# Plain fp32 products in column groups for the tokens over 128 of two gathered experts

## The reference

```python
def moe_ffn(u, w_router, b_router, w_gate, w_up, w_down):
    ...
    for e in range(N_EXPERTS):
        h = jax.nn.silu(u @ w_gate[e]) * (u @ w_up[e])
        y = y + gates[..., e:e + 1] * (h @ w_down[e]).astype(F32)
```

## Time and profile before

| | |
|---|---|
| median of 3 runs | 1476.37 us (1475.01 to 1477.93) |
| the profiled execution, its own time | 1475.07 us |
| its span | 1473.3 us |
| TensorE busy | 1402.8 us, 95% |
| VectorE busy | 807.9 us, 55% |
| ScalarE busy | 555.7 us, 38% |
| mean granted TensorE clock | 0.978 |
| mean DMA rate | 186 GB/s |
| ranks 2 and 3 | about 1048 to 1240 us of the span |
| ranks 4 to 7 | about 1240 to 1445 us |

### The profile page before, as it was taken

How to read it: one execution, slowest core, us unless ns; L and a number is a source line. 1 busy time by engine, 2 the same in 40 slices (tenths; PEclk the granted TensorE clock), 3 DMA queues, 4 the chain that set the end, 5 groups by cost and what they waited for, 6 DMA issues and landing times.

```text
span 1473.3 us, 20621 instructions
## 1 busy us (share of the span) xinstructions
PE 1402.8 (95%) x8551; PEld 1153.3 (78%) x8551; DVE 807.9 (55%) x1284; ACT 555.7 (38%) x721; POOL 23.6 (2%) x79
## 2 busy tenths in 40 slices
PE   6999999979999998999996999999999999999996
PEld 3678777679999966878774999999777676876664
DVE  1566315364444456641447534645545556899994
ACT  2351111154333235311104433334334345677762
POOL 6000000000000000000000000000000000000000
PEclk8999999989999999999997999999999999999999
DMA  9543764765545553445341724635656457999970
GB/s 321 180 143 126 250 200 152 260 196 172 159 152 165 171 160 114 144 160 189 112 126 44 242 90 154 220 104 180 196 177 205 148 188 230 315 343 339 353 245 32
DMA packets 205009, 274.75 MB, mean 186 GB/s; under 512 B 7783, under 2 KB 136065, under 8 KB 204916
## 3 DMA queue, kind: packets, MB, share of 16 engines
q1 hardware_dynamic: 192928, 262.57, 54.3%
q10 hardware_dynamic: 11988, 10.86, 2.3%
HBM read 267.11 MB, written 6.30 MB: 186 GB/s over the span
## 4 chain that ended last, share of the span: by engine, by line
PE 87%; DVE 7%; DMA 2%; ACT 2%; issue 1%; SPq 1%; DVEq 0%; ACTq 0%
PE bank L1002 17%; PE bank L871 10%; PE bank L873 9%; PE bank L872 9%; PE bank L901 8%; PE bank L902 8%; PE bank L903 8%; PE bank L949 2%; PE bank L1083 2%; PE bank L1095 1%; DMA out_dram<-SD 1%; PE bank L957 1%; PE bank L1091 1%; DMA raw<-in_w_ada_dram 1%; PE bank L1201 1%
## 5 line engine op out<-in xcount | busy, mean ns | idle before, releaser
L660 DVE TENSOR_TENSOR lo_raw<-raw,hi 128x2048 fp32r<-128x2048 f32 (+2 forms) x112 | 229.6, 2056 | 129.6 <-ACT hi L1487 129.0
L1487 ACT ACTIVATE hi<-raw 128x2048 fp32r<-128x2048 f32 (+2 forms) x112 | 193.5, 1728 | 136.0 <-PE bank L903 105.8
L1002 PE MATMUL bank<-UM,raw 128*128 128x288 f32 x896 | 228.2, 411 | 0.0
L871 PE MATMUL bank<-UH,hi 128*128 128x288 f32 x704 | 210.2, 299 | 9.2 <-DVE UL L1847 7.6
L1002 PEld LDWEIGHTS bank<-UM,raw 128*128 128x128 f32 x896 | 169.5, 192 | 50.3 <-issue 6.0
L873 PE MATMUL bank<-UL,hi 128*128 128x288 f32 x704 | 207.9, 295 | 0.0
L901 PE MATMUL bank<-hi,UGH 128*96 128x512 f32 (+7 forms) x384 | 144.5, 376 | 1.5 <-DVE XHF L2348 1.5
L903 PE MATMUL bank<-hi,UGL 128*96 128x512 f32 (+7 forms) x384 | 143.6, 374 | 0.0
L871 PEld LDWEIGHTS bank<-UH,hi 128*128 128x128 f32 x704 | 132.9, 189 | 9.5 <-issue 9.5
L873 PEld LDWEIGHTS bank<-UL,hi 128*128 128x128 f32 x704 | 133.3, 189 | 0.0
L872 PE MATMUL bank<-UH,lo 128*128 128x288 f32 x432 | 128.2, 297 | 0.0
(11 more groups left out here) (411 smaller groups left out, 2360.7 us busy)
## 6 DMA issues: line engine op xcount, KB each, us to landing
raw<-in_w_ada_dram SPq DMA_DIRECT2D x48, 1024.0 KB, 5.8
raw<-in_w_in_dram SPq DMA_DIRECT2D x28, 1024.0 KB, 7.7
raw<-in_w_exp_gate_dram SPq DMA_DIRECT2D x26, 1024.0 KB, 5.3
raw<-in_w_exp_up_dram SPq DMA_DIRECT2D x26, 1024.0 KB, 5.3
raw<-in_w_exp_down_dram SPq DMA_DIRECT2D x16, 1024.0 KB, 5.3
raw<-in_w_exp_down_dram SPq DMA_DIRECT2D x16, 768.0 KB, 4.6
raw<-in_w_ff_gate_dram SPq DMA_DIRECT2D x11, 1024.0 KB, 5.5
raw<-in_w_ff_up_dram SPq DMA_DIRECT2D x11, 1024.0 KB, 5.4
```

The lines of the kernel that those rows point to most:

```text
L660: dve.tensor_tensor(lo_x[g % XRAW][:, 0:XG[g][2] * XG[g][3]], x_raw(g), hi_x[g % XSPLIT][:, 0:XG[g][2] * XG[g][3]].bitcast(F32), ALU.subtr ...
L871: pe.matmul(out, wh, xh, start=start, stop=False)
L1002: mm = pe.matmul(bank[t][:, 0:N], w_[:, d, t * P:t * P + P], x_, start=(d == 0), stop=(d == KT - 1))
L1487: act.activation(hi_x[q][:, 0:XG[g][2] * XG[g][3]], x_raw(g), ACT.Copy).then_inc(S("x_hi_made"), 1)
```

## The change

The token tiles of ranks 2 and 3 are cut anew: a full tile of 128 tokens and a rest of 64 (rank 2, `SPREAD` 2) or 32 (rank 3, `SPREAD` 4; `CAPS` grows from 144 to 160). The full tile is computed as before. The rest is computed in plain fp32 from `raw` and from `UG` or `HRX` directly, without a split: the weight columns of a block are dealt over two groups of 64 or four groups of 32 array columns (`columns`), so that a k step is two matmuls of 256 moving columns or four of 128.

- `rest_block(g + 2)` is issued on TensorE before block g, since `x_lo` later overwrites `raw`. `x_lo` of these blocks waits for `rest_mm` and moves from step g - 3 to step g - 2 of VectorE (`lows_due`).
- The rest has its own Silu (ScalarE, steps 0, 4, 8), multiplication (VectorE, steps 2, 6, 10), transposes (`turn_rest`, after b = 3, 7, 11) and copy to `HRX` (ScalarE, steps 4, 8, 12). `boxes` gives the rectangles of the spread-out layout.
- `slot_masks` makes `ST` and `GSL` of the rest once for each group; `scatter` reads the rest from partitions 0, 32, 64 or 96 on.
- For all gathered experts `scatter` moves from after blocks 1, 4, 7, 10 to after 0, 2, 4, 6, and `add_slots` from steps 2, 5, 8, 11 to 1, 3, 5, 7.
- `UG` grows from 702 to 718 columns. The split of the tokens (`UGH`, `UGL`, `HHX`, `HLX`) covers the full tile only.

The diff, cut to its core:

```diff
 CAPS = [c + c % 2 for c in CAPS]
 SLOTS = []
 SLOT_OFF = {}
+SPREAD = []
 for _r in range(DENSE, NE):
     SLOT_OFF[_r] = sum(w_ for _, _, w_ in SLOTS)
-    _parts = -(-CAPS[_r] // P)
-    for _i in range(_parts):
-        SLOTS.append((_r, SLOT_OFF[_r] + _i * (CAPS[_r] // _parts), CAPS[_r] // _parts))
+    _rest = CAPS[_r] - P
+    assert _rest <= P // 2
+    SLOTS.append((_r, SLOT_OFF[_r], min(P, CAPS[_r])))
+    SPREAD.append(1)
+    if _rest > 0:
+        _rest = P // 4 if _rest <= P // 4 else P // 2
+        CAPS[_r] = P + _rest
+        SLOTS.append((_r, SLOT_OFF[_r] + P, _rest))
+        SPREAD.append(P // _rest)
...
+def columns(i, w_):
+    step = 512 // SPREAD[i]
+    return [(a, min(a + step, w_)) for a in range(0, w_, step)]
...
+REST = [g for g, t in enumerate(XG) if t[0] >= DENSE and len(TILES[t[0]]) > 1]
+REST_AHEAD = 2
+def lows_due(g):
+    return [x for x in (g + 2, g + 3) if x < NX and x - g == (2 if x in REST else 3)]
...
+            if g in REST:
+                dve.wait_ge(S("rest_mm"), REST.index(g) + 1)
             dve.tensor_tensor(lo_x[g % XRAW][:, 0:XG[g][2] * XG[g][3]], x_raw(g),
...
+            def rest_block(g):
+                r, b, kk, w_ = XG[g]
+                rs = r - DENSE
+                i = TILES[r][1]
+                n_ = SLOTS[i][2]
+                pe.wait_ge(S(f"x_full{g % XRAW}"), 16 * (g // XRAW + 1))
+                if g == REST[0]:
+                    pe.wait_ge(S("gb_made"), DENSE)
+                    pe.wait_ge(S("x_up_read"), DENSE * XCB)
+                if b < SUP:
+                    ci, up, half = b // 4, b // 2 % 2, b % 2
+                    x_, to = UG[:, 4 * half:4 * half + 4, SLOTS[i][1]:SLOTS[i][1] + n_], 2 * up + 1
+                    first, last = half == 0, half == 1
+                    if first and up:
+                        pe.wait_ge(S("rest_hf_made"), 3 * rs + ci)
+                    elif first:
+                        pe.wait_ge(S("rest_sg_made"), 3 * rs + ci)
+                        if ci == 0:
+                            pe.wait_ge(S("slot_hl_made"), 3 * rs)
+                            pe.wait_ge(S("rest_hx_made"), 3 * rs)
+                else:
+                    h, q = DOWN[b - SUP]
+                    x_, to = HRX[:, 4 * q:4 * q + kk, P:P + n_], (5 if h else 7)
+                    first, last = q == 0, q == 2
+                    pe.wait_ge(S("rest_hx_made"), 3 * rs + q + 1)
+                    if first and h == 0:
+                        pe.wait_ge(S("y_scaled"), DENSE * XDB)
+                        pe.wait_ge(S("sc_read"), 4 * rs)
+                    elif first:
+                        pe.wait_ge(S("slot_hl_made"), 3 * rs + 2)
+                w = x_raw(g).rearrange("p (k n) -> p k n", k=kk)
+                for k in range(kk):
+                    for q, (c0, c1) in enumerate(columns(i, w_)):
+                        mm = pe.matmul(bank[to][n_ * q:n_ * q + n_, 0:c1 - c0], x_[:, k, :], w[:, k, c0:c1],
+                                       start=first and k == 0, stop=last and k == kk - 1)
+                mm.then_inc(S("rest_mm"), 1)
+            def rest_due(g):
+                if g + REST_AHEAD in REST:
+                    rest_block(g + REST_AHEAD)
...
                         for c in range(NTT):
-                            pe.transpose(bank[6 + i % 2][0:w_, c * TT:c * TT + TT],
-                                         OH[:, c, off:off + w_].bitcast(F32), ident[0:TT, 0:TT])
+                            for q in range(SPREAD[i]):
+                                if SPREAD[i] == 1:
+                                    pe.transpose(bank[6 + i % 2][0:w_, c * TT:c * TT + TT],
+                                                 OH[:, c, off:off + w_].bitcast(F32), ident[0:TT, 0:TT])
+                                else:
+                                    pe.matmul(bank[6 + i % 2][w_ * q:w_ * q + w_, c * TT:c * TT + TT],
+                                              OH[:, c, off:off + w_].bitcast(F32), ident[0:TT, 0:TT], start=True, stop=True)
                         for c in range(NTT):
-                            mm = pe.matmul(bank[6 + i % 2][0:w_, N:N + 1], OH[:, c, off:off + w_].bitcast(F32),
-                                           GATR[:, c, r:r + 1], start=(c == 0), stop=(c == NTT - 1))
+                            for q in range(SPREAD[i]):
+                                mm = pe.matmul(bank[6 + i % 2][w_ * q:w_ * q + w_, N:N + 1], OH[:, c, off:off + w_].bitcast(F32),
+                                               GATR[:, c, r:r + 1], start=(c == 0), stop=(c == NTT - 1))
...
+                        rest_due(g)
                         pe.wait_ge(S("x_lo_made"), g + 1)
...
-                            for t, i in enumerate(TILES[r]):
-                                _, off, w_ = SLOTS[i]
-                                at_ = (f % 2) * CAPS[r] + off - w0
-                                mm = pe.transpose(bank[(0 if ci == 2 else 4) + f // 2][:, at_:at_ + w_],
-                                                  HFX[0:w_, t, f * P:f * P + P], ident[0:w_, 0:w_])
+                            mm = pe.transpose(bank[b0 + f // 2][:, f % 2 * w_:f % 2 * w_ + w_],
+                                              HFX[0:w_, 0, f * P:f * P + P], ident[0:w_, 0:w_])
...
+                    def turn_rest(r, ci):
+                        rs = r - DENSE
+                        i = TILES[r][1]
+                        pe.wait_ge(S("rest_hf_made"), 3 * rs + ci + 1)
+                        if ci == 0:
+                            pe.wait_ge(S("ysl_made"), halves_of(2 * rs))
+                        if ci == 1:
+                            pe.wait_ge(S("slot_hl_made"), 3 * rs + 1)
+                            pe.wait_ge(S("rest_hx_made"), 3 * rs + 1)
+                        if ci == 2:
+                            pe.wait_ge(S("slot_sg_made"), 3 * rs + 3)
+                        for j, fs in enumerate(rest_tiles(i, ci)):
+                            w_ = SLOTS[i][2] * len(fs)
+                            mm = pe.transpose(bank[(0 if ci == 2 else 4) + j][:, 2 * P:2 * P + w_],
+                                              HFX[0:w_, 1, j * P:j * P + P], ident[0:w_, 0:w_])
+                        mm.then_inc(S("rest_turned"), 1)
...
+                        for i in TILES[r][1:]:
+                            w_ = SLOTS[i][2]
+                            for x, b in enumerate(banks):
+                                d = 2 * pair + x
+                                step = 512 // SPREAD[i]
+                                q, c = d % 4 * P // step * w_, d // 4 * step + d * P % step
+                                pe.matmul(bank[b][:, 0:N], YSH[q:q + w_, 1, c:c + P], ST[q:q + w_, i, :], start=False, stop=False)
+                                mm = pe.matmul(bank[b][:, 0:N], YSL[q:q + w_, 1, c:c + P], ST[q:q + w_, i, :],
+                                               start=False, stop=True)
                         mm.then_inc(S("sc_full"), 1)
...
+                            n_ = SLOTS[TILES[r][0]][2]
+                            mm = slot_tiles(bank[2 * up][0:n_, 0:w_], g, UGH[:, 4 * half:4 * half + 4, 0:n_],
+                                            UGL[:, 4 * half:4 * half + 4, 0:n_], half == 0, half == 1)
...
-                        if rs > 0 and b in (1, 4, 7, 10):
-
-                            pair = b // 3
+                        if rs > 0 and b in (0, 2, 4, 6):
+                            pair = b // 2
                             pe.wait_ge(S("ysl_made"), halves_of(2 * rs - (1 if pair < 2 else 0)))
                             if pair > 0:
                                 pe.wait_ge(S("sc_read"), 4 * (rs - 1) + pair)
                             scatter(r - 1, pair, (6, 7))
+                        if len(TILES[r]) > 1 and b in (3, 7, 11):
+                            turn_rest(r, (b - 3) // 4)
...
+                            for v, w_, src in turned(r, ci):
+                                mm = act.activation(HHX[:, v, w_], src, ACT.Copy)
                             mm.then_inc(S("slot_hh_made"), 1)
+                        if len(TILES[r]) > 1 and b in (4, 8, 12):
+                            ci = b // 4 - 1
+                            i = TILES[r][1]
+                            act.wait_ge(S("rest_turned"), 3 * rs + ci + 1)
+                            for j, fs in enumerate(rest_tiles(i, ci)):
+                                n_ = SLOTS[i][2]
+                                mm = act.activation(HRX[:, 4 * ci + fs[0]:4 * ci + fs[-1] + 1:4 // SPREAD[i], P:P + n_],
+                                                    bank[(0 if ci == 2 else 4) + j][:, 2 * P:2 * P + n_ * len(fs)].rearrange(
+                                                        "p (f w) -> p f w", f=len(fs)), ACT.Copy)
+                            mm.then_inc(S("rest_hx_made"), 1)
+                        if len(TILES[r]) > 1 and b in (0, 4, 8):
+                            ci = b // 4
```

(23 more changed lines are left out.)

119 lines of the change are left out of this document (63 added, 56 removed).

## The result

The changed kernel takes **1435.39 us** (1434.92 to 1437.23, 4 runs) against 1475.86 us for the kernel before on the same chip (1475.01 to 1477.93, 4 runs): ratio 0.9726, 95% interval 0.9709 to 0.9743 (here and below a ratio is the time over that of the kernel before on the same chip; the brackets behind it are its 95% interval). The profiled execution took 1434.92 us, its span is 1432.8 us at a mean granted clock of 0.982, so 40.5 us less in the span.

The account below looks back on a forecast made before the run. TensorE bounds ranks 2 and 3; in ranks 4 to 7 VectorE and DMA are near full too. Terms sum to -35.9 us from 1475.07: 1439.2, plus 1.3 for the median, rounded 1440; range 1430 to 1462 (1430 to 1452: chance 0.68).

Parts of the forecast that it names:

- Second tiles, -91.8: Ranks 2 and 3: the second token tile's matmuls go, 45.9 us of TensorE for each expert, -91.8 us for both.
- Rests, +15.0 and +30.1: Rest products over 70 k steps each: rank 3 at 0.214 us a step, +15.0 us; rank 2 at 0.43, +30.1 us.
- rival of serial groups: Rank 2's rest: the two groups of 64 don't run side by side, +30.1 us, 1470 us; chance 0.08.
- Visits, +11.2: Going into column groups and back costs 0.31 us for each of 36 rest blocks, +11.2 us (bounds 7 and 22).
- rival of dear visits: Going into column groups and back costs 0.7 us instead of 0.31, 44 times: 17 us more, 1457 us; chance 0.12.
- Wider loads, +2.0: Full tiles with 128 tokens: 5 ns more for each of the 420 matmuls that stay, +2.0 us (0 to 3).
- Transposes, 0: Ranks 2 and 3: 44 transposes go, 22 wide ones and 9 of the rest come, about 3 us each way, 0.
- Scatter, +2.5: Scatter of ranks 2 and 3: rest rows start at other partitions, 0.31 us for each of eight pair groups, +2.5 us.
- Masks and gather, +1.6: Dense stage masks repeated over groups, about +1.2 us; gather with 16 more columns, 0.3 us; together +1.6 us.
- The earlier scatter, -5.0: Ranks 4 to 7: earlier additions remove TensorE's 6.3 us of stops at block 12, -5.0 us (0 to -6.3).
- The start of rank 2, -1.5: TensorE's 1.48 us wait for the last dense results is filled by the rest of block 2, -1.5 us.
- The lead: Rests two blocks ahead: VectorE may be 5.7 us late before TensorE stops; rival, lead too short, 1522 us, chance 0.05.

Follow-up runs that it names:

- experiment 5: Changed kernel with the rest of rank 3 in two groups of 256 columns instead of four of 128: 1450.24 us, ratio 0.9821.
- experiment 4: Changed kernel with the rest blocks issued in pairs ahead of every second full block, 18 visits instead of 36: 1430.59 us, ratio 0.9692.
- experiment 8: Changed kernel with each rest block cut in two, two k steps ahead of the full block and the others behind it: 1443.89 us, ratio 0.9786.
- experiment 7: Changed kernel with four rest blocks per visit (down product in pairs), 12 visits, VectorE's low halves behind its rest multiplication: 1431.01 us, ratio 0.969.
- experiment 1: Kernel before with only the earlier scatter (after blocks 0, 2, 4, 6; additions at steps 1, 3, 5, 7): 1468.91 us, ratio 0.9955.
- experiment 2: Changed kernel with scatter and additions of ranks 4 to 7 back at their old blocks, rank 3 staying early: 1443.75 us, ratio 0.978.
- experiment 6: Changed kernel with rest blocks one block ahead of the full tile instead of two, their low halves one step later: 1437.43 us, ratio 0.9736.
- experiment 3: Changed kernel with all k steps of one column group before those of the next in a rest block: 1469.19 us, ratio 0.9955.

## Why the prediction was right, and where it was off

The forecast was 1440 with -35.9 us; it came to 1435.4, and the spans differ by 40.5. The likeliest case is the one that happened, by its own mechanism. Of the 4.6 us between the two sums, 3.1 are the scatter: the gain of its move was sized too small, and its new rows were charged too much. The others are small sizes and two differences outside the changed stages that nearly cancel by luck: the profiled execution was 2.1 us earlier than forecast at the first dense product, and lost 1.7 us behind the last expert.

**Second tiles, -91.8: right.** In ranks 2 and 3 TensorE's time, from start to start, divides like this:

| us | before | after |
|---|---|---|
| products of the full tiles (before: both tiles) | 183.68 | 96.88 |
| rest | 0 | 45.01 |
| transposes | 2.94 | 4.56 |
| scatter | 4.29 | 5.40 |
| sum | 190.92 | 151.85 |

The 96.88 hold 4.9 us of entries and exits of the rest blocks (17 x 0.087 + 33 x 0.104), so 92.0 for the products themselves, half of 183.68.

**Rests, +15.0 and +30.1: right.** 0.2175 and 0.43 us for a k step: 15.2 and 30.1 us. The straight line between 128 and 512 columns was the right reading, for two groups of 64 too. The rival of serial groups is out, by the profile of the changed kernel itself; experiment 5 shows that the width of the groups doesn't matter.

**Visits, +11.2: right.** 0.30 us each by experiment 4 and again by 8. Read from the rows directly it is 0.09 before, 0.16 inside (0.14 in rank 3) and 0.10 behind, 0.35 where a 512-column product stands on either side. Behind a scatter it is only some 0.15, the part inside, since the other two are paid there without a visit as well: in experiment 4 a scatter that ends in products of 64 rows is followed 0.09 late by a full product too, and that one takes 0.34. Of the 17 visits saved in experiment 4, 13 stood between full products, at 0.335 to 0.35, and 4 behind a scatter: 13 x 0.345 + 4 x 0.15 = 5.1. For all 36 that gives 32 x 0.345 + 4 x 0.15 = 11.6 us, an estimate, where 36 x 0.30 would be 10.8; the forecast lies between. Its 0.31 came from small fp32 products of another part of the kernel. So the rival of dear visits is out. The Trainium skill (TensorEngine Tiling (Array Packing), Key Properties) has the engine drain at a change of the tiling mode; a loss of that kind is there at every visit, though no run shows that it is the drain. The 0.47 us that the prediction estimated from the skill's figures is half as much again as was measured.

**Wider loads, +2.0: 0.** With a stationary tile of 128 tokens the 512-column matmuls still follow each other after 0.231 us. The 5 ns that the forecast read from rank 4 were not the width. That window of 5.64 us begins behind four transposes, and the edge is what it paid for:

```profile
1258.54 0.47 PE L901 MATMUL bank<-hi,UGH 128*116 128x512 f32 x1
1258.85 0.40 PE L902 MATMUL bank<-lo_raw,UGH 128*116 128x512 f32 x1
```

The first product takes 0.31 us, the 23 behind it (5.64 - 0.31)/23 = 0.232 each.

**Transposes, 0: right, though the table has +1.6.** A group of four wide ones takes 0.53 us there, up to the start of the rest block behind it:

```profile
1079.46:1079.99 0.53, 0.53 (x4) 0.36 (x3) 1.00 0.00 0
```

The end of such a group is not the transposes' own. The two of the rest take 0.31 us in the changed kernel, where a rest block follows. In experiment 7 a full product follows directly. There it starts 0.14 us behind the first of the two, and takes 0.32 itself:

```profile
1069.56:1069.87 0.31, 0.31 (x2) 0.14 (x1) 1.00 0.00 0
```

```profile
1072.88 0.38 PE L1517 MATMUL bank<-ident,HFX 128*128 128x128 f32 x2
1073.01 0.48 PE L954 MATMUL bank<-hi,UGH 128*128 128x512 f32 x1
1073.33 0.40 PE L955 MATMUL bank<-lo_raw,UGH 128*128 128x512 f32 x1
```

So 0.17 us at the end of each of the 12 turns, 2.1 in all, are the entry of the visit behind it, and a full product there would have paid 0.09 for the edge anyway. Less the 0.17, four wide transposes take 0.36 us, 0.09 each (an estimate: no run has a full product directly behind four wide ones), near the 0.083 of the forecast.

**Scatter, +2.5: +1.5.** The four pair groups of rank 2 take 1.36 us instead of 1.08, 0.28 for the change from 128 to 64 rows and back. Those of rank 3 stay at 1.09. There the stationary operands of the two 32-row products of a pair lie in different rows, and the two run side by side (they start 0.007 and 0.003 us apart in these rows):

```profile
1207.42 0.40 PE L1529 MATMUL bank<-ST,YSH 32*128 32x288 f32 x2
1207.66 0.29 PE L1530 MATMUL bank<-ST,YSL 32*128 32x288 f32 x2
1207.88 0.49 PE L954 MATMUL bank<-hi,UGH 128*116 128x512 f32 x1
```

That saves about as much as the change of rows costs. The product behind them takes 0.33 us instead of 0.23, so they add the other 0.4 us in rank 4: ranks 4 to 7 take 197.6 us where experiment 1 has 197.2.

**Masks and gather, +1.6: right within what can be told.** From the first dense product to rank 2 it was forecast as 3 x (1.72 + 0.31) + 1.3 - 1.5 = +5.9 us, and it is +5.5, in experiment 2 as well. In it the masks' matmuls take 7.39 us instead of 6.55, start to start, +0.8 where the forecast had about 1.2. The gather, ahead of this stage, takes 19.8 and 20.2 us in the two traces without the wider `UG` and 20.1 to 20.6 in the nine with it; the forecast of +0.3 is inside that spread.

**The earlier scatter, -5.0: -7.** This is the term that was most undersized. VectorE and DMA took nothing back, though they are all but full; and a stop costs 0.22 us more than its idle time. With the scatter of rank 3 cheaper as well (0.4 us where 1.25 were charged), ranks 4 to 7 came out 3.1 us under the forecast.

**The start of rank 2, -1.5: right**, and with the same edge a little more; experiments 7 and 8 bring the stop back, each with another order around it.

**The lead: right.** No stop in 36 blocks; experiment 6 shows that even one block of lead costs nothing. `x_lo` does wait 46 us for the rest, as the rival had it, on an engine with the time for it; only with the rest behind the block (experiment 8) did TensorE stop for it.

**What the sum didn't have: +1.7 behind the last expert.** The same 16 products of the closing variance take longer. Windows over that place, of the kernel before and of the kernel after:

```profile
1455.00:1461.00 6.00, 4.01 (x16) 2.82 (x16) 1.91 (x4) 2.70 (x5) 0.00 (x0) 1.00 0.00 0
```

```profile
1413.30:1419.30 6.00, 5.21 (x15) 3.43 (x13) 0.54 (x1) 1.99 (x4) 0.00 (x0) 0.72 0.00 0
```

The granted clock is 0.72 there instead of 1.00, so a part of it runs at the lower of TensorE's two levels, 1.2 instead of 2.4 GHz. In both kernels alike 4 us stand ahead of it in which TensorE is busy for 1.85. Over the 16 products themselves it is 1.00 before and in experiments 1 and 5, where they take 4.12 us, and 0.71 or 0.72 in all the other traces, where they take 5.7 to 5.8. Experiment 5 is a variant of the changed kernel, so the change by itself doesn't bring the +1.7. What decides between the two was not tried.

The sum by stretches. The forecast for ranks 2 and 3 holds the rests and visits that lie there (58 and 70 k steps and 33 visits) and rank 2's scatter:

| stretch | forecast | measured | difference |
|---|---|---|---|
| up to the first dense product | +0.3 | -1.8 | -2.1 |
| dense experts | +5.9 | +5.5 | -0.4 |
| ranks 2 and 3 | -38.4 | -39.1 | -0.7 |
| ranks 4 to 7 | -3.8 | -6.9 | -3.1 |
| behind the experts | 0 | +1.7 | +1.7 |
| sum | -35.9 | -40.5 | -4.6 |

The first difference is put down to chance: up to there the two traces with the old order (before and experiment 1) differ by 0.7 us between themselves, and those of the changed kernel and its variants by up to 2.6. The rows are rounded.

**The best version** that the runs showed is the one in pairs, 1430.59 us, 3.1% under the kernel before; the one by chunks can't be told from it.

## What to carry to other kernels

When a few rows over 128 cost a whole second pass of the array, compute them in column groups and price it by three numbers: k steps times the moving columns of one group, a fixed price for every entry, and the lead that the other engines need. The fixed price is the one to work on: put neighbouring visits together until the work that is moved ahead opens a gap somewhere else, as it did here from 18 to 12 visits. And count a stop of TensorE from start to start, not by its idle time: here one was 0.22 us longer than its row says, and the four together 1.0 us longer.

## What the runs showed of the hardware

In these runs plain fp32 matmuls to one column group started ahead of matmuls to another group that stand before them in the program, ahead of three but not of four. With runs of four instructions a group the next group began 0.013 us behind the first (rest block 1.93 us, 1.88 interleaved). With runs of eight it began with the fifth (2.79 us, and 2.39 in rank 3), where serial groups would give 3.6 us by the expectation of experiment 3. The Trainium skill (TensorE: Matmul & The Clock Gate, The mechanism) has matmuls start and end in the order of the program; for the starts the measurement differs here, and it decides. No run here shows the order of the ends. So products for several groups needn't be interleaved one by one: runs of four instructions cost 0.04 to 0.05 us a block, and runs of eight 0.9 to 1.4.
